# Attention's bias on ScalarE with v evicted ahead of the last head's norm, and the state-space part's own and neighbour terms as products summed by ones

## The reference

```python
# attention: a query sees the topk = 128 keys with the highest index score (blocks of 128 queries)
score = jnp.where(visible[None], score, -jnp.inf)
_, idx = lax.top_k(score, topk)
logits = jnp.einsum('bqhd,bqkhd->bhqk', qb, k_sel) * scale
logits = jnp.where(valid[:, None], logits, -jnp.inf)
p = jax.nn.softmax(logits, axis=-1)

# state space: S_t = diag(f_t) S_{t-1} + k_t v_t^T, o_t = S_t^T q_t
b = jnp.cumsum(chunks(log_f), axis=3)
A = jnp.einsum('bhtd,bhsd,bhtsd->bhts', qc, kc, decay)   # decay[t,s,d] = exp(b_t - b_s), s <= t
intra = jnp.einsum('bhts,bhse->bhte', A, vc)
```

## Time and profile before

| | us |
|---|---|
| median of 3 runs | 2335.97 |
| profiled execution, its own time | 2333.98 |
| profiled execution, its span | 2332.2 |
| PE busy | 2273.7 (97%) |
| VectorE busy | 1007.9 (43%) |
| ScalarE busy | 613.0 (26%) |
| GpSimd busy | 1459.9 (63%) |

### The profile page before, as it was taken

How to read it: one execution, slowest core, us unless ns; L and a number is a source line. 1 busy time by engine, 2 the same in 40 slices (tenths; PEclk the granted TensorE clock), 3 DMA queues, 4 the chain that set the end, 5 groups by cost and what they waited for, 6 DMA issues and landing times.

```text
span 2332.2 us, 30970 instructions
## 1 busy us (share of the span) xinstructions
PE 2273.7 (97%) x11139; PEld 1841.0 (79%) x11139; DVE 1007.9 (43%) x1598; ACT 613.0 (26%) x1083; POOL 1459.9 (63%) x1452
## 2 busy tenths in 40 slices
PE   8999999999999999999999999999999889999999
PEld 7767887888888887678878888888977557888887
DVE  6975553532331049657535333211384453333200
ACT  4333324221110023343242211110244552111100
POOL 6644665876667756546648767667493236767663
PEclk9999999999999999999999999999999999999999
DMA  5321333322332233212334232232330102332232
GB/s 183 100 72 55 95 103 112 133 97 93 99 99 92 98 116 101 72 55 95 96 117 137 91 99 98 91 99 92 121 114 16 37 1 77 104 99 95 94 100 81
DMA packets 69861, 217.37 MB, mean 93 GB/s; under 512 B 8448, under 2 KB 10752, under 8 KB 69632
## 3 DMA queue, kind: packets, MB, share of 16 engines
q1 hardware_dynamic: 54016, 188.41, 25.2%
q10 hardware_dynamic: 15744, 27.52, 3.3%
HBM read 195.93 MB, written 10.49 MB: 89 GB/s over the span
## 4 chain that ended last, share of the span: by engine, by line
PE 90%; DVE 6%; ACT 2%; issue 1%; ACTq 0%; DMA 0%; POOL 0%; DVEq 0%; POOLq 0%
PE ps L1665 78%; PE ps L1985 2%; PE ps L2150 2%; DVE score L1449 1%; DVE small L1445 1%; PE ps L1931 1%; ACT pe L1013 1%; PE ps L1916 1%; PE ps L2210 1%; PE ps L2170 1%; PE ps L1944 1%; PE ps L2028 1%; PE ps L2212 1%; PE ps L2015 0%; PE ps L2079 0%
## 5 line engine op out<-in xcount | busy, mean ns | idle before, releaser
L536 POOL TENSOR_TENSOR w_lo<-w_raw,w_hi 128x512 fp32r<-128x512 f32 x700 | 951.4, 1359 | 58.4
L533 POOL TENSOR_SCALAR w_hi<-w_raw 128x512 fp32r<-128x512 f32 x700 | 487.0, 696 | 680.1 <-DMA w_raw<-wst 651.3
L1665 PE MATMUL ps<-h_hi,w_lo 128*128 128x512 f32 (+1 forms) x2056 | 803.8, 391 | 20.0 <-issue 4.9
L1665 PE MATMUL ps<-h_lo,w_hi 128*128 128x512 f32 (+1 forms) x2056 | 784.9, 382 | 0.0
L1665 PE MATMUL ps<-h_hi,w_hi 128*128 128x512 f32 (+1 forms) x2056 | 784.8, 382 | 0.0
L1665 PEld LDWEIGHTS ps<-h_hi,w_lo 128*128 128x128 f32 x2056 | 387.5, 188 | 121.0 <-issue 33.4
L1665 PEld LDWEIGHTS ps<-h_lo,w_hi 128*128 128x128 f32 x2056 | 387.9, 189 | 77.7 <-issue 6.2
L1665 PEld LDWEIGHTS ps<-h_hi,w_hi 128*128 128x128 f32 x2056 | 387.4, 188 | 75.4
L1665 PE MATMUL ps<-a_hi,w_lo 128*128 128x512 f32 (+1 forms) x572 | 213.7, 374 | 0.0
L1665 PE MATMUL ps<-a_hi,w_hi 128*128 128x512 f32 (+1 forms) x572 | 213.2, 373 | 0.0
L1665 PE MATMUL ps<-a_lo,w_hi 128*128 128x512 f32 (+1 forms) x572 | 213.2, 373 | 0.0
(11 more groups left out here) (301 smaller groups left out, 2570.5 us busy)
## 6 DMA issues: line engine op xcount, KB each, us to landing
w_raw<-wst SPq DMA_DIRECT2D x350, 512.0 KB, 3.5
rot<-raw ACTq DMA_DIRECT2D x70, 128.0 KB, 3.3
gates<-gt ACTq DMA_DIRECT2D x32, 256.0 KB, 4.2
stage<-gates ACTq DMA_DIRECT2D x32, 256.0 KB, 3.0
x_sb<-xin SPq DMA_DIRECT2D x8, 256.0 KB, 5.6
out<-x_sb SPq DMA_DIRECT2D x8, 256.0 KB, 4.5
kc<-cst ACTq DMA_DIRECT2D x1, 1056.0 KB, 4.9
kc<-cst SPq DMA_DIRECT2D x1, 417.0 KB, 8.0
```

The lines of the kernel that those rows point to most:

```text
L533: eng.tensor_scalar(w_hi[s][:, part], w_raw[s][:, part], 1.0, 1.0, ALU.mult, ALU.mult)\
L536: eng.tensor_tensor(w_lo[s][:, part], w_raw[s][:, part], w_hi[s][:, part].bitcast(F32), ALU.subtract)\
L1665: m = eng.matmul(o, w, x, start=first and i == 0, stop=final and i == 2)
```

## The change

Attention: ScalarE evicts v0 to v3 before `qk_norm(7)`, not after. The bias is made by ScalarE, in `bias(b)`, ahead of the eviction of f3: for the first query block a Copy of the causal mask times -1, for the other three Relu(score * 5e-9 + 1e30), which is 0 where the mark -3e38 stands and 1e30 elsewhere; it waits for VectorE's last MATCH_REPLACE8 on that block. VectorE subtracts it where it added before; its three TENSOR_SCALAR go.

State space: level 0 is now VectorE's product f * q over 2048 columns, summed over the 128 channels by a stationary matrix of ones: 4 matmuls of 512 columns. Level 1 is the same with exp(b) * q * k at the odd tokens: 4 matmuls of 256 columns, read with a step of two elements. Every row of the result is the same, and the masked copy takes from it what it took before. The exponent of level 1 and its first Exp go, the 16 masked copies of level 0 become one. Level 8's multiplication is split, so that the last block's queries are kept unscaled in `q_last`. For each head six matmuls become four (two of them 256 columns wide), and ten become seven (a stationary block of v serves its own block and, in one matmul, all later ones).

```diff
@@ ScalarE, attention
-                qk_norm(7)
                 for t in range(TB):
                     free(eng.activation(v_sb[:, t, :], acc((l, f"v{t}")), ACT.Copy), (l, f"v{t}"))
+                qk_norm(7)
+
+                def bias(b):
+
+                    dst = bias_t[:, BOFF[b]:BOFF[b] + NKEYS[b]]
+                    if b == 0:
+                        eng.activation(dst, causal, ACT.Copy, scale=-1.0).then_inc(bias_ready, 1)
+                        return
+                    eng.wait_ge(topk_done, 3 * l + b)
+                    eng.activation(dst, score[:, b - 1, 0:NKEYS[b]], ACT.Relu, scale=NEG / -2.0e38, bias=far)\
+                       .then_inc(bias_ready, 1)
+
                 for i in range(4):
+                    if i == 3:
+                        for b in range(TB):
+                            bias(b)
                     free(eng.activation(f_sb[:, i, :], acc((l, f"f{i}")), ACT.Copy), (l, f"f{i}"))
@@ ScalarE, decay(j)
-                    eng.wait_ge(lvd, 9 * l + j)
+                    if j == 1:
+                        eng.wait_ge(prep_v, 2 * l + 2)
+                    else:
+                        eng.wait_ge(lvd, 8 * l + j - 1)
...
-                        step(eng.activation(xa, xa, ACT.Exp))
+                        if j > 1:
+                            step(eng.activation(xa, xa, ACT.Exp))
                         eng.activation(xb, bb, ACT.Exp).then_inc(lve, 1)
@@ VectorE, selection
-                            last[b] = step(eng.match_replace(s, m8[b], s, MARK))
+                            ins = eng.match_replace(s, m8[b], s, MARK)
+                            if j == TOPK // 8 - 1:
+                                ins.then_inc(topk_done, 1)
+                            else:
+                                last[b] = step(ins)
                     rope(3 + i)
-                for b in (1, 2, 3):
-                    after(last[b])
-                    k = step(eng.tensor_scalar(bias_t[:, BOFF[b]:BOFF[b] + NKEYS[b]], score[:, b - 1, 0:NKEYS[b]],
-                                               -2.0e38, NEG, ALU.is_gt, ALU.mult))
-                after(k)
...
+                        if p == 0 and i == 0:
+                            eng.wait_ge(bias_ready, 4 * l + b + 1)
@@ VectorE, weigh(j)
+                        if j == 1:
+                            after(step(eng.tensor_tensor(xb, xb, qb, ALU.mult)))
+                            eng.tensor_tensor(xb, xb, ka, ALU.mult).then_inc(lvx, 1)
+                            return
...
+                    elif j == 8:
+                        step(eng.tensor_tensor(xl[0][:, :, 0:3 * P], xl[0][:, :, 0:3 * P], hq_sb[:, :, 0:3 * P], ALU.mult))
+                        eng.tensor_tensor(q_last[:, :, :], xl[0][:, :, 3 * P:T], hq_sb[:, :, 3 * P:T], ALU.mult)\
+                           .then_inc(lvx, 1)
...
-                eng.wait_ge(prep_v, 2 * l + 2)
-                exponent(1)
                 eng.wait_ge(prep_a, 3 * l + 3)
...
-                eng.tensor_copy(small[:, 112:113], small[:, 126:127]).then_inc(keys_ready, 1)
                 eng.wait_ge(hq_ready, l + 1)
+                eng.tensor_tensor(xf[0], fl, qf, ALU.mult).then_inc(keys_ready, 1)
                 weigh(1)
...
-                        m = ident.bitcast(I32)
-                        for n in range(16):
-                            ins = eng.copy_predicated(af[:, n * P:(n + 1) * P], m, ps[:, 1024 + n * P:1024 + (n + 1) * P])
-                            if n < 15:
-                                step(ins)
+                        m = ident.bitcast(I32).rearrange("p (o t) -> p o t", o=1).to_broadcast([P, 16, P])
+                        ins = eng.copy_predicated(af.rearrange("p (n t) -> p n t", t=P), m,
+                                                  ps[:, 1024:1024 + 16 * P].rearrange("p (n t) -> p n t", t=P))
...
-                eng.tensor_tensor(qe3[:, :, :], q4, et[:, :, 2:3].to_broadcast([P, HH, P]), ALU.mult).then_inc(tail_ready, 1)
+                eng.tensor_tensor(q4, q_last[:, :, :], et[:, :, 2:3].to_broadcast([P, HH, P]), ALU.mult).then_inc(tail_ready, 1)
@@ TensorE, level(i)
+                    if i <= 1:
+                        for h in range(HH):
+                            x = xl[i][:, h, i::i + 1]
+                            n = T // (i + 1)
+                            m = eng.matmul(ps[:, 1024 + n * h:1024 + n * (h + 1)], ones, x, start=True, stop=True)
+                        m.then_inc(lv_mm, 1)
+                        return
@@ TensorE, heads
+                    keys = [xl[1][:, h, a * P:(a + 1) * P] for a in range(3)]
+                    later = xl[0][:, h, 2 * P:4 * P]
+                    o = 512 * (2 + 2 * (h % 2))
+                    for lo, ke, qe in ((0, keys[0], xl[0][:, h, P:2 * P]), (1, ke0[:, h, :], later),
+                                       (3, keys[2], q_last[:, h, :]), (4, keys[1], later)):
+                        m = eng.matmul(ps[:, o + lo * P:o + lo * P + qe.shape[-1]], ke, qe, start=True, stop=True)
...
+                    behind = (slice(0, 3 * P), slice(4 * P, 6 * P), slice(3 * P, 4 * P))
+                    for a in range(TB):
+                        vt = hv_sb[:, a, h * P:(h + 1) * P]
+                        m = eng.matmul(bank(6 + h % 2, a * P, P), vt, a_sb[:, h, a * P:(a + 1) * P],
+                                       start=a == 0, stop=a == TB - 1)
+                        if a < TB - 1:
+                            eng.matmul(bank(6 + h % 2, (a + 1) * P, T - (a + 1) * P), vt, cross[h % 2][:, behind[a]],
+                                       start=False, stop=False)
```

More of the change, by code:

```diff
@@ L269, in program @@
         cross = [sbt(f"cross{i}", WK + 80 + 3 * i, 768) for i in range(2)]
-        ke0, qe3 = sbt("ke0", WK + 86, 4, P), sbt("qe3", WK + 88, 4, P)
+        ke0, q_last = sbt("ke0", WK + 86, 4, P), sbt("q_last", WK + 88, 4, P)
         gt = [sbt(f"gt{i}", WK + 64 + 2 * i, T) for i in range(2)]
@@ L331, in program @@
         eps = small[:, 127:128]
+        far = small[:, 125:126]
         def sem(name):
@@ L369, in program @@
         relu_used = sem("relu_used")
+        topk_done = sem("topk_done")
+        bias_ready = sem("bias_ready")
         s_ready = sem("s_ready")
@@ L1092, in _ @@
             step(eng.memset(eps, EPS))
+            step(eng.memset(far, -NEG))
             eng.wait_ge(in_dma, 32)
@@ L1441, in _ @@
                 for i in range(8):
-                    for _ in range(2):
+                    for j in (2 * i, 2 * i + 1):
                         for b in (1, 2, 3):
@@ L1463, in _ @@
                         eng.wait_ge(s_ready, 32 * l + 8 * p + n + 1)
+                        if p == 0 and i == 0:
+                            eng.wait_ge(bias_ready, 4 * l + b + 1)
                         eng.tensor_tensor_reduce(p_sb[i][:, b, 0:nk], bank(SCORE_BANKS[b % 2][i], 0, nk),
                                                  bias_t[:, BOFF[b]:BOFF[b] + nk], 1.0, MARK,
-                                                 ALU.add, ALU.max, small[:, n:n + 1]).then_inc(s_taken, 1)
+                                                 ALU.subtract, ALU.max, small[:, n:n + 1]).then_inc(s_taken, 1)
                     eng.wait_ge(s_taken, 32 * l + 8 * p + 8)
@@ L1529, in exponent @@
                     elif j == 9:
-                        eng.wait_ge(lvd, 9 * l + 8)
+                        eng.wait_ge(lvd, 8 * l + 7)
                         b3 = bf.rearrange("p (n t) -> p n t", t=P)
@@ L1540, in weigh @@
                         (xa, xb), (ka, _), (_, qb) = halves(x, j), halves(fl, j), halves(qf, j)
+                        if j == 1:
+                            after(step(eng.tensor_tensor(xb, xb, qb, ALU.mult)))
+                            eng.tensor_tensor(xb, xb, ka, ALU.mult).then_inc(lvx, 1)
+                            return
                         step(eng.tensor_tensor(xa, xa, ka, ALU.mult))
                         eng.tensor_tensor(xb, xb, qb, ALU.mult).then_inc(lvx, 1)
[L1543 to L1547 removed]
+                    elif j == 8:
+                        step(eng.tensor_tensor(xl[0][:, :, 0:3 * P], xl[0][:, :, 0:3 * P], hq_sb[:, :, 0:3 * P], ALU.mult))
+                        eng.tensor_tensor(q_last[:, :, :], xl[0][:, :, 3 * P:T], hq_sb[:, :, 3 * P:T], ALU.mult)\
+                           .then_inc(lvx, 1)
+                    else:
+                        eng.tensor_tensor(x, x, fl, ALU.mult).then_inc(lvx, 1)
                 eng.wait_ge(prep_a, 3 * l + 3)
@@ L1975, in level @@
                         eng.wait_ge(lv_taken, 8 * l + max(1, i - 1))
-                    w = 1 << max(i - 1, 0)
-                    for n in range(16):
[L1978 to L1987, removed]
+                    if i <= 1:
[5 more added lines that the diff above has]
+                        return
+                    w = 1 << (i - 1)
+                    for n in range(16):
+                        x = xl[i % 2][:, n // TB, n % TB * P:n % TB * P + P]
```

(15 more changed lines are left out.)

1 line of the change is left out of this document (removed).

## The result

The changed kernel takes 2321.39 us, the median of 6 runs (2314.80 to 2327.35), beside 2337.29 us for the kernel before (6 runs, 2335.08 to 2340.38). The ratio is 0.9932, with a 95% interval of 0.9915 to 0.9949: 15.9 us faster, where 15.8 was forecast. The interval goes from 11.9 to 19.9 us, and the median of before was 1.3 us higher in this comparison than the one the forecast started from, so the agreement to 0.1 us is luck; the median itself is 1.2 us above the forecast 2320.2. The profiled execution took 2321.99 us, its span 2320.2; TensorE (PE) is busy for 2266.9 us of it (98%).

What follows compares the result with a forecast made beforehand. TensorE, busy 97%, was taken as the bound. Attention 7.1, layer 0's levels 2.6, layer 1's 5.8 and heads 0.3 gave 15.8 us off 2333.98: 2318.2, plus 2.0 for the median, 2320.2 us; range 2315.5 to 2327.

Steps and rivals of the forecast that it cites:

- v and the later arrival: Before the first scores: of 2.0 and 3.6 us PE regains, 0.8 and 0.45 go into waiting for the last rope.
- The bias on ScalarE: First scores: VectorE loses 3.30 us of bias in layer 0; ScalarE's bias ends by 953.3, covered by 1.0 us.
- The first scores: Attention, both layers: scores take 2.98 us, ending 3.9 and 3.2 us earlier, 7.1 together with v's part.
- rival 1: Clock falls at the first scores, 1.6 us each: 2321.8 us in one layer, 2323.4 in both; chance 0.23.
- Levels 0 and 1, the copy, the product: State space: level 0 3.5 us, level 1 1.95, masked copy 2.5, VectorE's product 2.60 and hidden.
- Rival 2: State space: slow wide copy (5.1 us) gives 2329.4 us, half-rate step of two alone 2323.8; chance 0.15.
- Heads: Wider matmuls per head: 0.03 us saved per head and kind, 0.3 us in all at most.
- rival 3: Layer 1's clock falls were an accident of the profiled execution, never lost in the median: 2325.0 us; chance 0.07.
- I take the fall as gone: Layer 1's level 1 and its gate: shorter wait and dense matmuls end the clock fall; 3.0 + 2.0 = 5.0 us saved.
- One clock fall instead of four: Sign expected in the profile after: only one of the trace's four falls to 1.2 GHz remains.
- Rival 4: Clock falls at thin levels 2 to 7, 3.2 us each: 2342.6 us with seven, 2358.6 with all 12; chance 0.03.

Runs made afterwards that it cites:

- second profile: Profile from running the changed kernel again with no edit: median 2317.85 us, ratio 0.9927 to the kernel before; the profiled execution took 2316.21 us.
- the ones in the wait: Changed kernel with 10 (layer 0) and 6 (layer 1) ones-by-ones products ahead of TensorE's wait for the last rope: 2318.71 us, ratio 0.9924 to the kernel before.

## Why the prediction was right, point by point

**v and the later arrival.** Right. The wait for v is gone, and PE waits for the last rope instead. The forecast had it idle 1.6 and 1.3 us there; the profile of the changed kernel shows at most 3.1 and 1.75, its second profile at most 1.2 in each layer. Adding up the stalls would have promised 4.0 for v alone; v alone gave 2.3 in the rest.

**The bias on ScalarE.** Hidden, as forecast, but with less room. ScalarE in layer 0 of the changed kernel:

```profile
135.52 1.91 ACT L798 ACTIVATE bias_t<-score,small 128x256 f32<-128x256 f32 x3 [3.51 <-DVE score L1471]
137.34 0.58 ACT L805 ACTIVATE f_sb<-ps 128x512 f32<-128x512 f32 x1
```

The eviction of f3 stood directly behind the three Relus, so it was they that set it, not f3's own end. It was done at 137.9, still 1.8 us before the rope. The forecast's bound of 0.85 us for one Relu was safe (0.51 to 0.73 for one, 1.91 for three). What the move is worth was read from an uncommon execution: the 1.60 us that PE waited for VectorE's bias in the earlier trace rows came with GpSimd's instructions beside it, and in four later traces of the same lines, where GpSimd had a gap, PE waited 0.25 us. So a part of the 7.1 us was a matter of which execution was read.

**The first scores.** 2.98 us at full clock was right (2.92 in the second profile). In the profiled execution of the changed kernel the clock fell in both layers, rival 1 in its stronger form; in the six other traces with v ahead it fell in neither. What brings it stays open: the ones in the wait did not settle whether the longer wait does.

**Levels 0 and 1, the copy, the product.** Right to 0.1 us each. The copy took the rate of level 3 (2.62 us for 2048 columns, line 1590), not 5.1. Level 1 read its columns with a step of two at the full rate: four matmuls of 256 in 2.05 us with their start, where the sum had 1.95. The Trainium skill (SBUF — State Buffer, Door 1: The DMA port swizzle) says that two accesses to each line of 16 bytes are enough for the full rate; the trace agrees, with these 2.05 us. Rival 2 is out. The product took 2.29 to 2.59 us (2.60 forecast) and nobody waited for it.

**Heads.** 0.3 forecast, about 0.6 found: the matmuls between blocks take 1.31 in place of 1.34 us and the output's 2.18 in place of 2.23, so 0.08 for each of 8 heads.

**The sum in its two parts.** At equal clock the forecast is 15.8 less the falls that it counted: 1.6 at layer 1's f products, 3.2 at its level 1, and 1.4 at layer 0's scores (3.20 us for a group that takes 1.83 at full clock). That is 9.6; the rest fell by 9.5 (2322.9 to 2313.4 on one chip, standard error 0.6); alone, the attention edits gave 3.7 (4.1 forecast) and the state-space edits 5.0 (5.5 forecast). For the clock 6.2 us were forecast; the loss fell by 8.2 on that chip (standard error 1.6). A part of it is level 1's: the state-space edits lowered the loss by 2.4 and 4.7 us in two comparisons, and no level 1 of the new form fell in 14 places. So rival 3 (the falls never were in the medians) is out for level 1, and the step "I take the fall as gone" was right there. Its size was partly luck: the forecast counted one fall per execution from one trace, and the next trace had two. The attention edits alone (1.3) and the state-space edits alone (2.4) sum to 3.7 of loss on another chip, not to 8.2; where the difference comes from stays open.

**Where it was wrong.** "One clock fall instead of four" did not come true: the profile has four, at other places in part (one at 391 us, before the merge of layer 0, that no profile of the kernel before had). Its second profile has two, and neither has one at f0. The forecast gave the fall at layer 1's f0 as part of v's gain (1.6 us). The mean of v alone can't judge this: its loss is 1.1 above before with a standard error of 1.9. The count of the traces speaks for it (9 falls in 14 places with v behind the norm, none in 14 with v ahead), but chip and form are not kept apart there, so it leans to the forecast and is not shown. The falls ahead of the merge came only with the state-space edits (4 of 14 against 0 of 14); each stood behind a wait of 1.88 to 3.05 us, and of the 24 others of these places only three waited as long (1.90, 1.93 and 2.08). No step of the forecast had them, and why the wait grew was not tried. Rival 4, falls at the thin levels 2 to 7, did not occur in any profile.

What stays open: how the loss of 5 to 6 us that the changed kernel keeps is shared out. Its first profile lost 8.5 us in its four stretches and its second 3.4 in two; both have one of 3.4 us in the second block, and the other traces show stretches of up to 10.2 us at that place, where no kernel has an edit. A filling of those waits was not tried.

## What to carry to other kernels

When two waits stand one behind the other, price the removal of the first by the later of the next arrivals; here v alone gave 2.3 of 4.0 us. A wait read from one trace may be that execution's: the 1.60 us for the bias were 0.25 in four others, so read the same lines in a second trace before you price them. A short wait of TensorE ahead of thin matmuls (here 64 columns, which take as long as 128) can cost more than itself: give the wait cheap products (4.5 us faster), or make what follows dense (the loss 4.7 lower). Where one kernel's runs scatter, split each time into the loss to the clock and the rest: here effects of 1 to 5 us could be told apart in a scatter of 12.

## What the runs showed of the hardware that was not expected

Five products of ones by ones (1.1 us) in a wait of 1.1 us ahead of thin matmuls made the kernel 4.5 us faster. One and the same kernel lost between 2.3 and 13.9 us to the clock from one execution to the next, with rests from 2311.8 to 2313.8. A masked copy's rate hangs on the length of its runs: for 1024 columns 2.54 us in runs of one and 1.30 in runs of four, and 2.62 us for 2048 columns in runs of 128. VectorE's TENSOR_SCALAR from SBUF to SBUF takes longer the more GpSimd works beside it: three of 256, 384 and 512 columns took 0.89 us with GpSimd idle, 2.20 with it busy for 1.8 us of them and 3.30 with it busy for 2.9.
